# Multiplications of identity and ones on the matrix engine, ahead of its long waits

## What is computed

```python
mod = cond @ w_ada[l] + b_ada[l]
sh_m, sc_m, gt_m, sh_f, sc_f, gt_f = jnp.split(mod, 6, axis=-1)
h = rms_norm(x, g_pre_mix[l]) * (1 + sc_m[:, None, :]) + sh_m[:, None, :]
proj = h @ w_in[l]
...
x = x + gt_m[:, None, :] * rms_norm(mix @ w_out[l], g_post_mix[l])
h = rms_norm(x, g_pre_ffn[l]) * (1 + sc_f[:, None, :]) + sh_f[:, None, :]
y = moe_ffn(h, w_router[l], b_router[l], w_gate_up[l], b_gate_up[l], w_down[l], b_down[l])
x = x + gt_f[:, None, :] * rms_norm(y, g_post_ffn[l])
```

## Time and profile before

| | |
|---|---|
| three runs | 2083.15, 2078.98, 2082.37 us |
| median | 2082.37 us |
| the profiled execution | 2081.78 us |
| its span, from the first to the last instruction | 2080.0 us |
| TensorE matmuls | 1946.8 us busy, 94% of the span |
| mean granted clock of TensorE | 0.98 |
| DMA | 609.34 MB, mean 293 GB/s |

### The profile page before, as it was taken

The page is one execution under the profiler, slowest core; times in us unless marked ns, Lnnn a source line. Parts: engine busy times, 40 slices in busy tenths (PEclk is TensorE's granted clock), DMA queues, the critical chain, the costliest instruction groups (busy, mean ns, idle before and its releaser), DMA issues.

```text
span 2080.0 us, 28166 instructions
## 1 busy us (share of the span) xinstructions
PE 1946.8 (94%) x10657; PEld 1196.4 (58%) x10658; DVE 893.4 (43%) x1381; ACT 722.3 (35%) x1181; POOL 585.1 (28%) x622
## 2 busy tenths in 40 slices
PE   4998699999999999999998989999999999999998
PEld 1885333332333333333332259889888798898887
DVE  2553421111222221122211147557788566576983
ACT  1453211111111111111111145664665456646662
POOL 3400224433434334334334403000143022001340
PEclk7999899999999999999999989999999999999999
DMA  9958799999898999989999975356456553554653
GB/s 356 317 184 350 310 373 417 419 417 417 337 417 354 396 418 418 419 355 419 418 418 417 419 248 203 122 162 202 138 186 208 169 196 123 182 170 136 195 190 120
DMA packets 203045, 609.34 MB, mean 293 GB/s; under 512 B 10459, under 2 KB 115055, under 8 KB 166385
## 3 DMA queue, kind: packets, MB, share of 16 engines
q1 hardware_dynamic: 197360, 585.14, 73.8%
q0 software_dynamic: 5280, 22.19, 3.0%
q10 hardware_dynamic: 328, 0.95, 0.1%
HBM read 607.17 MB, written 9.26 MB: 296 GB/s over the span
## 4 chain that ended last, share of the span: by engine, by line
PE 71%; DMA 11%; SPq 6%; DVE 5%; ACT 4%; issue 2%; POOL 1%; ACTq 0%; DVEq 0%
PE bank L852 21%; PE bank L1184 15%; PE bank L889 10%; PE bank L1208 9%; DMA side<-in_w_gate_up 8%; PE bank L891 5%; SPq L694 4%; PE bank L1135 3%; SPq L701 2%; PE bank L1148 1%; DMA ring<-in_w_down 1%; PE bank L959 1%; PE bank L1176 1%; DVE split L1631 1%; PE bank L984 1%
## 5 line engine op out<-in xcount | busy, mean ns | idle before, releaser
L1184 PE MATMUL bank<-ring,qkv 128*64 128x512 f32 x2240 | 502.4, 597 | 33.0 <-POOL ring L2349 33.0
L1184 PEld LDWEIGHTS bank<-ring,qkv 128*64 128x64 f32 x2240 | 152.0, 137 | 365.4 <-issue 266.2
L1631 DVE TENSOR_TENSOR split<-ring,split 128x2048 fp32r<-128x2048 f32 x104 | 249.4, 2398 | 115.9 <-ACT split L2068 115.8
L889 PE MATMUL bank<-hT_both,split 128*128 128x512 f32 x800 | 283.6, 398 | 7.1 <-DVE split L1631 7.1
L1208 PE MATMUL bank<-ring,qkv 128*64 128x512 f32 x1120 | 248.5, 595 | 1.4 <-DMA ring<-in_w_down 1.1
L2068 ACT ACTIVATE split<-ring 128x2048 fp32r<-128x2048 f32 x104 | 199.2, 1916 | 131.0 <-PE bank L852 126.2
L891 PE MATMUL bank<-hT_both,split 128*128 128x256 f32 x800 | 225.4, 282 | 0.0
L1605 DVE TENSOR_SCALAR qkv<-bank 128x512 f32<-128x512 f32 x35 | 24.2, 692 | 442.5 <-PE bank L1184 442.5
L2040 ACT ACTIVATE qkv<-qkv 128x512 f32<-128x512 f32 x35 | 22.1, 630 | 532.1 <-DVE qkv L1605 532.1
L1619 DVE SCALAR_TENSOR_TENSOR out_halves<-bank,small,out_halves 64x512 fp32r<-64x512 f32 x70 | 52.5, 750 | 326.6 <-ACT out_halves L2051 326.1
L889 PEld LDWEIGHTS bank<-hT_both,split 128*128 128x128 f32 x800 | 151.4, 189 | 43.6 <-DVE split L1631 8.3
(11 more groups left out here) (359 smaller groups left out, 3046.1 us busy)
## 6 DMA issues: line engine op xcount, KB each, us to landing
ring<-in_w_down SPq DMA_DIRECT2D x150, 1024.0 KB, 17.2
ring<-in_w_gate_up SPq DMA_DIRECT2D x70, 1024.0 KB, 19.9
probs<-in_w_gate_up SPq DMA_DIRECT2D x62, 1024.0 KB, 17.9
ring<-in_w_in SPq DMA_DIRECT2D x58, 1024.0 KB, 5.6
ring<-in_w_up SPq DMA_DIRECT2D x44, 1024.0 KB, 5.1
consts<-in_w_gate_up SPq DMA_DIRECT2D x31, 1024.0 KB, 20.5
side<-in_w_gate_up SPq DMA_DIRECT2D x31, 1024.0 KB, 22.5
qkv<-in_w_gate_up SPq DMA_DIRECT2D x31, 1024.0 KB, 21.7
```

The lines of the kernel that those rows point to most:

```text
L889: pe.matmul(b[:, :].rearrange("p (h t) -> p h t", h=2), w_high[:, k, rows], hT_both[:, :, k, :], start=(k == 0), stop=False, skip_group_ch ...
L1184: last = pe.matmul(hidden[q][CAP * j:CAP * j + CAP, :], xgT[:, k % 4, k // 4, :], unit_at(k)[:, c:c + 512], start=False, stop=(k == KC - 1 ...
L1631: dve.tensor_tensor(low, unit_at(u % RING_L), high.bitcast(F32), ALU.subtract).then_inc(low_done, 1)
```

## The change

A helper `keep_awake(b, n)` is added, which multiplies the identity by 64 columns of ones n times into a bank `b`. It is called at twelve points of TensorE's program, 174 matmuls in all: 6 after each of the units 3 to 7 of `ada(0)`, 32 before the first wait for `h_ready`, 12 after `turn_h`, 28 before the product with `w_out`, 10 before the rows of `ada(2)`, 28 before the second wait for `h_ready`, 14 before the wait for the chosen experts, and 20 after the last `scatter`. Each result is overwritten by the next tile of that bank, which starts a new sum. No other engine's program changes.

```diff
+            def keep_awake(b, n):
+
+                for _ in range(n):
+                    pe.matmul(b[:, 0:DH], ident, ones[:, 0:DH], start=True, stop=True)
+
@@
                     used(last)
+                    if r == 0 and 3 <= k:
+                        keep_awake(take("mod0"), 6)
@@
+            keep_awake(take("h0"), 32)
             for tt in range(TT):
                 pe.wait_ge(h_ready, seen(h_ready))
             turn_h([f"h{j}" for j in range(4)], htok)
+            keep_awake(take(IN1[0]), 12)
             read(*[f"h{j}" for j in range(4)])
@@
+            keep_awake(take("mix0"), 28)
             split_rows_product("mix", lambda f: (mix_hi[:, f, :], mix_lo[:, f, :]), KC, mixed_in)
             ada_units(2, range(KC // 2, KC))
+            keep_awake(take("mod8"), 10)
             ada_rows(2)
+            keep_awake(take("g0"), 28)
@@
-            pe.wait_ge(route_ready, 1)
             b = take("places")
+            keep_awake(b, 14)
+            pe.wait_ge(route_ready, 1)
@@
             scatter(True)
+            keep_awake(turn_bank, 20)
```

More of the change, by code:

```diff
@@ L1085, in _ @@
             tile(last)
+            b = take("places")
+            keep_awake(b, 14)
             pe.wait_ge(route_ready, 1)
-            b = take("places")
             before = const("before")
```

## The result

The changed kernel is slower. Its four runs took 2100.15 us in the median (2097.34 to 2103.27), beside 2082.76 us (2078.98 to 2085.77) for the kernel before: a ratio of 1.0074, with a 95% interval of 1.0058 to 1.0089 (the ratios in this document come from the comparison of all runs and need not equal the quotient of the two medians). The profiled execution took 2103.27 us, its span 2101.5 us against 2080.0 us. The forecast was 2080.1 us with a range up to 2085.0 us; the time lies 15 us above that range.

What follows compares the result with a forecast made beforehand. TensorE's cold clock after waits was taken as the bound, about 2.1 us per cold start on the path; 1.65 - 1.45 - 1.5 + 0.3 - 1.3 = -2.3 us from 2082.37 gave 2080.1 us, range 2075.5 to 2085.0 us.

Steps and rivals of the forecast that it cites:

- They keep the engine loaded about as a run of transposes does: All added matmuls: they load TensorE enough to hold or raise its clock, at 0.23 us each.
- rival 3: All added runs: 64-column matmuls too thin to hold the clock, 0.42 us each, +25 us, 2107 us; chance 0.08.
- First block: Up to the projections: second projection pays the cold start instead of the first; +1.65 us, bounds -0.35 and +2.3.
- no unit starts late: Units of ada(0): six added matmuls, 1.4 us, lie within 1.42 us idle, and the clock stays up.
- Product with `w_out`: Product with w_out: starts 0.45 us late, saves 1.9 us of cold time; -1.45 us, bounds -1.9 and -0.9.
- Rows and second turn: Rows of ada(2) and second turn: added matmuls fit the waits, work runs warm; -1.5 us, bounds -1.7 and -0.6.
- Routing: Routing: 14 added matmuls overrun by 0.4 us, small tiles gain 0.1 us, gather stays cold at 3.36 us; +0.3 us.
- Layer's entry: Entry of the layer: 20 added matmuls warm the transposes and 48 records; -1.3 us, bounds -1.6 and 0.
- the first five to eight cold: Layer's entry: of 20 added matmuls only the first five to eight run at the lower clock, 0.42 us each.
- The sum: Whole kernel: the terms by place add to -2.3 us, giving 2080.1 us; this forecast held chance 0.40.
- nothing absorbs a shift from the routing on: From the routing through the expert loop: time won or lost ahead of the loop stays to the end.
- every idle time of 2.7 us or more in these rows ended cold: TensorE's waits: argument that the clock falls before the second projection, which then pays a cold start, + 2.0 us.

Runs made afterwards that it cites:

- e8_wide_kept: The changed kernel with 256 columns, the first block's three places left out, places before attention a's scores and each layer's fourth gate unit added: 2077.59 us, ratio 0.9963.
- e1_wide: The changed kernel with half as many added matmuls, each of 256 columns in place of 64: 2084.83 us, ratio 1.0004 to the kernel before.
- e7_128: The changed kernel with 128 columns in place of 64, same number and places: 2083.73 us in one run, beside 2085.33 us of before.
- e2_transposes: The changed kernel with two transposes of ones in place of each added matmul: 2089.72 us in one run, beside 2084.84 us of before.
- e5_halved: The changed kernel with every count of added matmuls halved, still 64 columns: 2087.28 us, ratio 1.0005 to the kernel before.

## Why the prediction was wrong

**The step that failed** is the sentence "They keep the engine loaded about as a run of transposes does; that this is enough I take from the second turn". The price was taken from transposes too (0.23 us for two records), and that was right: 6.46 us for 28. But records of equal length did not do the same to the clock. A record of a transpose moves 128 columns in 0.116 us, one of the added matmuls 64 columns in 0.115 us. In the runs, 128 columns and transposes held the clock through the run of 32 before the first turn; 64 columns did not, with ones or with dense values. I saw a row that spoke for this (32 rows of the bias product ran cold, though busy) and let the turn outweigh it, with 0.08 for the case that came.

**What followed from it** was rival 3, with its mechanism but not all of its sizes. It took 0.42 us for a cold matmul (0.43). It had overruns of 6, 5, 3 and 3 us on the path and 8 us at the first projections. Measured: none at the product, 4.0 at the second turn, 3.6 from the router to block 0, 1.5 at the layer's entry, 10.6 at the first projections; 21.5 us between the profiled executions, 17.4 and 12.9 us between the medians of the two comparisons, for its 25. It did not name the units of `ada(0)`: six cold matmuls take 2.75 us in an idle time of 1.42 us, beside a unit that is itself 0.87 us longer.

**First block.** The claim that "no unit starts late" fell with the clock. The rest of that paragraph is confirmed where the clock holds: a new idle time before the second projection (5.59 us for 4.2), cold behind it, +2.58 us for +1.65. With 128 columns the clock held through that gap in one profile, and the same stretch came out at -0.08 us, the case that the prediction bounded by -0.35; in the other it was +0.87 us. So in these three profiles the places of the first block, 74 of 174 matmuls, won at most 0.08 us and lost up to 2.6 us with the clock up at the turn: the halves of the second projection's weights still set its start (56.57 and 56.02 us with 128 columns, 57.23 us with 256).

**Product with `w_out`.** Right, wherever matmuls were added there: -1.7 to -1.8 us for the product itself, where half of the cold 3.9 us had been put at 1.9. With the 0.44 us of the row above, which had been put at 0.45, the changed kernel has -1.38 for -1.45.

**Rows and second turn.** -1.5 us is what the 256 columns gave (-1.47). With 64 it was +4.0 us.

**Routing.** The gather stayed cold, at 3.68 us (3.4 foreseen). The overrun of 14 matmuls was 1.3 us, not 0.4, since the clock fell inside them.

**Layer's entry.** The clock was down before the added matmuls, as foreseen, but "the first five to eight cold" was wrong: all 20 were, 8.63 us for a wait of 5.39. In `e8_wide_kept` it came up inside the 11 and stayed. In `e1_wide` it was down again from 1229 to 1236 us, over the 48 records, so that place brought 0.60 us there and 0.9 us in `e8_wide_kept`.

**The sum.** With the clock held, the -2.3 us were not confirmed either: the 256-column version is level with before (1.0004, 0.9989 to 1.0019), and so is the 128-column one (1.0003, 0.9991 to 1.0015). In the profile with 256 columns the sum is +3.60 us, and the largest misses are in the layers and between the projections and the product, where nothing is added; as far as they are known these are differences between executions.

**What carries to the end.** That nothing absorbs a shift from the routing on holds: 13.2 us at the router had become 21.5 us at the end, and the first block's shift came through the loop whole. Idle time didn't decide alone, however: "every idle time of 2.7 us or more in these rows ended cold" is true of before and not of `e7_128`, where 2.68 us before the same scores and 2.69 us before the second projection ended at 1.00; and idle times of 1.4 and 0.8 us were followed by the lower clock in `e2_transposes` and by the upper one in before.

## What to carry to other kernels

Filling a wait of the matrix engine paid here where the filler (the added matmuls) held the clock and where the work behind it was bound by the matrix engine and not by a transfer. Judge a filler by the granted clock in the windows, not by busy time, and measure it before relying on it; of two that cost the same, as 64 and 128 columns do here, try the wider. If the clock may fall, the count is what limits the loss: counts that fit the wait even at the lower clock (`e5_halved`) cost next to nothing, though they won nothing. Where the traces show it, a place was worth 0.9 to 1.7 us, so seven chosen places made 0.4%, and twelve with the narrow width lost 0.7%.

## What the runs showed of the hardware

- A TensorE that is listed as busy in 34.90 of 34.90 us had its clock at 0.51. Busy time doesn't tell whether the clock is held.
- A float32 matmul on 128x128 weights takes 0.23 us with 64 and with 128 columns (6.46 us for 28, 7.34 us for 32) and 0.45 us with 256 (6.74 us for 15, with its tail), at the upper clock; with 64 columns at the lower clock it takes 0.43 us (13.81 us for 32).
- The Trainium skill, "TensorE: Matmul & The Clock Gate", Part 1, "HAM oscillation — how this bites in real kernels", puts the swings of the clock in a matmul kernel with few rows down to a wait for data at every tile. Here there was no wait within the runs of 64 columns, and the clock fell inside them (13.81 us for 32 matmuls).
- 64 transposes in a row held the clock at its upper level for 7.15 us (1.00). In the same execution 32 others ran at 0.50 for 5.6 us before it rose.
- The same instructions see the clock fall at 24 us in two executions and at 33 us in a third, which moves the second 96 records of projections by some 5 us (+10.56 and +10.48 us against +5.75).
